# Moving the rotated rows of the rotary embedding: from a TensorE matmul to transfers inside SBUF, issued from the weight-load queue

## The chip, the cores and the metric

The kernel runs on one core of a Trainium2 chip. The metric is the device time of one execution in microseconds; a number for a kernel is the median of several executions. Lower is better.

## The reference

Two layers of a first kind, then two of a second kind, on a sequence of 512 tokens and a width of 1024. Only the first kind is touched. Each such layer projects x with `w_in`, turns four of the projected parts (queries and key of the sparse attention, queries and key of its index) by the rotary embedding, and goes on with three kinds of attention, a merge, a feed-forward part and normalizations.

```python
def rope(x, pos):
    half = x.shape[-1] // 2
    inv = ROPE_THETA ** (-jnp.arange(half, dtype=jnp.float32) / half)
    ang = pos.astype(jnp.float32)[:, None] * inv[None, :]
    cos, sin = ...                      # of ang, broadcast over heads
    x1, x2 = x[..., :half], x[..., half:]
    return jnp.concatenate([x1 * cos - x2 * sin, x2 * cos + x1 * sin], axis=-1)

for i in range(DEPTH):                  # first_block, DEPTH = 2
    h = x @ w_in[i]
    (fq, fk, fv, ff_logit, sq, sk, sv, dq, dk, dv, iq, ik, iw, g) = split_cols(h)
    ...
    dq, dk, iq, ik = rope(dq), rope(dk), rope(iq), rope(ik)    # heads of 64
    o_dsa = dsa_attention(dq, dk, dv, iq, ik, iw)
    ...
```

A rotated row is the row of the other half of the same head of 64: row r is paired with row r XOR 32, and the pairing carries a minus sign for the lower half.

## The kernel before

Everything is kept with features on partitions and the 512 tokens along the free dimension. Weights come in *units*: 1024 inputs by 128 outputs, one transfer of 512 KB into one of four buffers `w_raw`. ScalarE splits a unit into a rounded part `w_hi` (`act_split`, L396), GpSimd computes the rest `w_lo` (`pool_split`, L411), and TensorE multiplies a unit in 24 matmuls (`pe_tile`, L387 to L389: eight input tiles, three products each) into the PSUM bank of the unit's slot, unit number modulo 4. ScalarE then takes the bank into the tile `proj` (L1149, `take`) and at once splits the raw unit four places further on. There is no planner: each engine has a program in a fixed order, and semaphores tie them together.

The semaphores that matter: `bank_free[s]` counts that ScalarE has emptied the bank of slot s, so the projected tile stands in `proj`; `lo_ready[s]` counts that GpSimd is through with `w_raw[s]`, so that the next unit may be loaded into it; `unit_done[s]` counts that TensorE has finished a unit; `rope_done` counts tiles that VectorE has turned.

SyncE's queue, `sp_stream`, only loads weights: in a loop over groups of four units it waits for `lo_ready[s]` and issues the load of unit v, which means that unit v-4 has been split, which happens when unit v-8 has been taken out of its bank.

The projection of a first-kind layer is 25 units, in the order `A_ORDER`. The nine tiles to be turned, `ROPE`, are exactly its first nine, so tile n of `ROPE` is unit n. Three of them use 64 partitions, six use 128. `ROT_AT` says after which unit TensorE makes which rotated tiles: two after units 3, 5, 7 and 9, one after unit 10. Each is a matmul with a constant 128x128 matrix of +1 and -1 (L997), into the PSUM bank `X[n % 2]`. VectorE multiplies the tile by the cosine (L1389), the bank by the sine (L1390), and adds (L1392). The first wait for a rotated tile also releases the two VectorE operations ahead of them (L1381, L1383) that prepare the forget gate of another attention part.

Unit 0 and 1 (in the second layer unit 0, 1 and 2) are multiplied side by side, so they end close together; all later units one after another.

Of the kernel before, what the change touches and what calls it, by code (L numbers as in the profile page):

```python
# [20 lines left out]
ALU = mybir.AluOpType  # L21
# [3 lines left out]
P = 128  # L25
SEQ = 512
# [3 lines left out]
HD = 64  # L30
SLOTS = 4
DEPTH = 2
# [19 lines left out]
A_GROUPS = A_UNITS // SLOTS  # L52
# [4 lines left out]
A_ORDER = (16, 17, 18, 20, 21, 22, 23, 24, 25, 0, 1, 2, 3, 4, 5, 6, 7, 8, 9, 10, 11, 12, 13, 14, 15)  # L57
A_SPARE = 25

ROT_AT = {3: (0, 1), 5: (2, 3), 7: (4, 5), 9: (6, 7), 10: (8,)}  # L60
VT_AT = {11: (0, 1), 13: (2, 3), 15: (4, 5), 23: (6,)}
# [10 lines left out]
C_ID, C_ROT, C_TRI, C_CAUS, C_STRICT, C_ST01, C_CHUNK = (P * n for n in range(7))  # L72
# [37 lines left out]
def plan(nc, ctx):  # L110

    S = Plan()
# [99 lines left out]
    def sem(name):  # L212
        return ctx.enter_context(nc.semaphore(name))
# [10 lines left out]
    S.dup_ready = sem("dup_ready")  # L224
    S.rot_ready = sem("rot_ready")
    S.rope_done = sem("rope_done")
# [170 lines left out]


def sp_stream(S, sp, w_dram, groups):

    with sp.Fori(1, groups) as g:
        for s in range(SLOTS):
            sp.wait_ge(S.lo_ready[s], g)
            src = w_dram[bass.ds(g * SLOTS + s, 1), :, :].rearrange("a p n -> (a p) n")
            sp.dma_start(S.raw[s][:, :], src).then_inc(S.raw_landed[s], 16)

# [539 lines left out]
def GA(L, u, i=0):  # L946

    return L * A_GROUPS + u // SLOTS + i
# [33 lines left out]
def a_tensor(S, pe):  # L982
    nc = S.nc
    ident = S.con[:, C_ID:C_ID + P]
    for L in range(DEPTH):
        G = lambda u, i=0: L * A_GROUPS + u // SLOTS + i

        def taken(tile):
            u = A_ORDER.index(tile)
            pe.wait_ge(S.bank_free[u % SLOTS], G(u) + 2)  # L990

        def rot(n):
            tile = ROPE[n][0]
            taken(tile)
            if n >= 2:
                pe.wait_ge(S.rope_done, L * len(ROPE) + n - 1)
            nc.tensor.matmul(S.X[n % 2][:, :], S.con[:, C_ROT:C_ROT + P], S.qkv[:, tile * SEQ:(tile + 1) * SEQ],  # L997
                             start=True, stop=True).then_inc(S.rot_ready, 1)

        def turn_v(v):  # L1000
# [14 lines left out]
        for u in range(wide, len(A_ORDER)):  # L1015
            pe_unit(S, pe, u, G(u), S.ps[u % SLOTS][:, :], S.xh, S.xl).then_inc(S.unit_done[u % SLOTS], 1)
            if L == 0 and u == min(ROT_AT):
                pe.wait_ge(S.con_landed, 16 * 5)
            for n in ROT_AT.get(u, ()):
                rot(n)  # L1020
            for v in VT_AT.get(u, ()):
                turn_v(v)
# [49 lines left out]
        for i in range(2):  # L1072
            for jj in range(4):
                u = A_UP + jj
# [297 lines left out]
def a_vector(S, dve):  # L1372
    nc = S.nc
    for L in range(DEPTH):
# [3 lines left out]

        dve.wait_ge(S.rot_ready, L * len(ROPE) + 1)
        f, na = S.c[64:128, :], S.wk[5][64:128, :]  # L1380
# [4 lines left out]
        for n, (u, lo, hi) in enumerate(ROPE):  # L1385
            t = S.qkv[lo:hi, u * SEQ:(u + 1) * SEQ]
            a, b = S.wk[n % 2][lo:hi, :], S.wk[2 + n % 2][lo:hi, :]
            dve.wait_ge(S.rot_ready, L * len(ROPE) + n + 1)
            nc.vector.tensor_tensor(a, t, S.cos[lo:hi, :], ALU.mult)  # L1389
            nc.vector.tensor_tensor(b, S.X[n % 2][lo:hi, :], S.sin[lo:hi, :], ALU.mult)  # L1390
            dve.drain()
            nc.vector.tensor_tensor(t, a, b, ALU.add).then_inc(S.rope_done, 1)  # L1392
# [1098 lines left out]
def rope_constants():  # L2491
    inv = np.float32(10000.0) ** (-np.arange(32, dtype=np.float32) / np.float32(32))
    ang = (np.arange(SEQ, dtype=np.float32)[:, None] * inv[None, :]).astype(np.float32)
    rep = lambda t: np.ascontiguousarray(np.tile(t.T, (4, 1)).astype(np.float32))
    return rep(np.cos(ang)), rep(np.sin(ang))

# [31 lines left out]
```

## Time and profile before

| | us |
|---|---|
| median of 3 runs | 2758.76 (2757.78 to 2759.20) |
| the profiled execution, its own time | 2759.12 |
| its span, first to last instruction | 2757.3 |
| TensorE busy in the span | 2670.7 (97%) |
| VectorE, ScalarE, GpSimd busy | 1448.3, 1143.9, 1061.0 |

The busy time of TensorE is a modelled one, since matmuls overlap; what one matmul costs is read from the distance between starts, or between the takings of two banks. The span lies 1.8 us below the execution's own time, which is 0.36 us above the median.

### The profile page before, as it was taken

The page shows a single profiled execution, that of the slowest core. Times are in us where ns is not written, and L with a number is a line of the kernel's source. Part 1 is how long each engine was busy: PE and PEld are TensorE (multiplying, and loading weights), DVE is VectorE, ACT ScalarE, POOL GpSimd, SP SyncE. Part 2 cuts the span into 40 slices and gives each one's busy share as a digit, 9 for nine tenths or more (in the row PEclk, how much of TensorE's full clock was granted, in tenths as well). Part 3 has the DMA queues.
Part 4 walks back from the last instruction along what each step waited for, and adds up shares of the span by engine and source line. Part 5 has one row for each costly group of instructions (what it writes and reads, how often), then busy time and mean ns, then how long its engine had stood idle before and what let it go on. Part 6 is the DMA issues. An engine that isn't in the chain of part 4 may idle for free.

```text
span 2757.3 us, 35837 instructions
## 1 busy us (share of the span) xinstructions
PE 2670.7 (97%) x12688; PEld 2034.4 (74%) x12688; DVE 1448.3 (53%) x2434; ACT 1143.9 (41%) x1984; POOL 1061.0 (38%) x430
## 2 busy tenths in 40 slices
PE   8999999999999999999999999999999999999998
PEld 6867666688888778676667888886787766887766
DVE  5237647463223252486374533233688764688764
ACT  2344445243223342454444332324336554337554
POOL 4332123344444334321133444453346622347612
PEclk9999999999999999999999999999999999999999
DMA  4221111233332222211122322232133211233211
GB/s 162 91 77 54 47 46 62 77 99 94 97 99 91 84 76 85 76 54 45 40 77 77 107 92 91 94 104 76 61 103 119 85 39 54 76 98 120 72 40 54
DMA packets 61322, 220.33 MB, mean 80 GB/s; under 512 B 6928, under 2 KB 7056, under 8 KB 61200
## 3 DMA queue, kind: packets, MB, share of 16 engines
q1 hardware_dynamic: 60624, 217.12, 24.5%
q8 instruction: 78, 1.28, 0.2%
q10 hardware_dynamic: 576, 1.57, 0.2%
q14 instruction: 44, 0.36, 0.0%
HBM read 216.57 MB, written 2.10 MB: 79 GB/s over the span
## 4 chain that ended last, share of the span: by engine, by line
PE 92%; DVE 3%; ACT 2%; POOL 1%; DVEq 1%; issue 1%; DMA 0%; ACTq 0%; SPq 0%
PE bank L387 25%; PE bank L389 24%; PE bank L388 24%; PE bank L501 3%; PE bank L528 3%; PE bank L514 2%; PE bank L850 1%; PE bank L716 1%; POOL w_lo L411 1%; PE bank L504 1%; PE bank L708 1%; PE bank L734 1%; PE bank L1033 1%; PE bank L738 1%; PE bank L997 1%
## 5 line engine op out<-in xcount | busy, mean ns | idle before, releaser
L411 POOL TENSOR_TENSOR w_lo<-w_raw,w_hi 128x1024 fp32r<-128x1024 f32 x404 | 1010.4, 2509 | 1666.8 <-ACT w_hi L396 1660.9
L387 PE MATMUL bank<-x_hi,w_hi 128*128 128x512 f32 x2112 | 872.7, 413 | 30.7 <-DVE x_lo L2324 11.0
L389 PE MATMUL bank<-x_hi,w_lo 128*128 128x512 f32 x2112 | 830.7, 393 | 0.0
L388 PE MATMUL bank<-x_lo,w_hi 128*128 128x512 f32 x2112 | 829.4, 393 | 0.0
L396 ACT ACTIVATE w_hi<-w_raw 128x1024 fp32r<-128x1024 f32 x400 | 419.5, 1055 | 437.9 <-PE bank L389 376.0
L387 PEld LDWEIGHTS bank<-x_hi,w_hi 128*128 128x128 f32 x2112 | 400.4, 190 | 147.4 <-issue 49.3
L389 PEld LDWEIGHTS bank<-x_hi,w_lo 128*128 128x128 f32 x2112 | 399.9, 189 | 86.5
L388 PEld LDWEIGHTS bank<-x_lo,w_hi 128*128 128x128 f32 x2112 | 401.4, 190 | 78.9 <-issue 7.2
L387 PE MATMUL bank<-rhs_hi,w_hi 128*128 128x512 f32 x624 | 245.9, 394 | 6.1 <-DVE rhs_lo L1472 6.1
L388 PE MATMUL bank<-rhs_lo,w_hi 128*128 128x512 f32 x624 | 244.2, 391 | 0.0
L389 PE MATMUL bank<-rhs_hi,w_lo 128*128 128x512 f32 x624 | 243.9, 391 | 0.0
L558 ACT ACTIVATE work<-bank,neg_max 128x128 f32<-128x128 f32 (+3 forms) x216 | 112.0, 523 | 210.4 <-DVE neg_max L586 174.5
L1537 DVE TENSOR_TENSOR ffn_sum<-ffn_sum,bank 128x512 f32 x64 | 43.9, 688 | 286.1 <-PE bank L389 286.1
L2094 DVE SCALAR_TENSOR_TENSOR bank<-glu_out,params_b_cur,bank 128x512 f32<-128x512 f32 x216 | 152.7, 752 | 35.1 <-issue 35.1
L1527 DVE TENSOR_TENSOR work<-work 128x512 f32<-128x512 f32 x64 | 90.9, 1420 | 139.6 <-ACT rhs_hi L1292 139.6
L387 PEld LDWEIGHTS bank<-rhs_hi,w_hi 128*128 128x128 f32 x624 | 117.7, 189 | 36.2 <-issue 11.7
L389 PEld LDWEIGHTS bank<-rhs_hi,w_lo 128*128 128x128 f32 x624 | 118.0, 189 | 24.7
L388 PEld LDWEIGHTS bank<-rhs_lo,w_hi 128*128 128x128 f32 x624 | 118.0, 189 | 23.9
L586 DVE TENSOR_REDUCE neg_max<-bank 128x1 f32<-128x128 f32 (+3 forms) x216 | 96.1, 484 | 64.2 <-PE bank L504 62.6
L1290 ACT ACTIVATE work<-bank 128x512 f32<-128x512 f32 x64 | 38.0, 594 | 193.3 <-PE bank L389 185.1
L1149 ACT ACTIVATE proj<-bank 128x512 f32<-128x512 f32 x50 | 29.9, 597 | 201.7 <-PE bank L389 201.7
L567 ACT ACTIVATE work<-bank 128x128 f32<-128x128 f32 (+3 forms) x216 | 82.8, 437 | 41.9 <-PE bank L528 32.7
(391 smaller groups left out, 3257.7 us busy)
## 6 DMA issues: line engine op xcount, KB each, us to landing
w_raw<-w SPq DMA_DIRECT2D x404, 512.0 KB, 3.5
ln_in<-x SPq DMA_DIRECT2D x4, 512.0 KB, 7.4
out<-residual SPq DMA_DIRECT2D x8, 256.0 KB, 2.2
p_raw<-p ACTq DMA_DIRECT2D x2, 512.0 KB, 3.6
constants<-con SPq DMA_DIRECT2D x1, 455.0 KB, 10.3
cos<-cos SPq DMA_DIRECT2D x1, 256.0 KB, 10.4
sin<-sin SPq DMA_DIRECT2D x1, 256.0 KB, 10.2
params_b<-prm_b ACTq DMA_DIRECT2D x1, 256.0 KB, 3.7
```

Source lines behind the costliest of these rows:

```text
L387: nc.tensor.matmul(out, wh, xh, start=first, stop=False)
L388: nc.tensor.matmul(out, wh, xl, start=False, stop=False)
L389: S.last = nc.tensor.matmul(out, wl, xh, start=False, stop=last)
L396: S.nc.scalar.activation(S.wh[s][:, :], S.raw[s][:, :], ACT.Copy).then_inc(S.hi_ready[s], 1)
L411: S.nc.gpsimd.tensor_tensor(S.wl[s][:, :], S.raw[s][:, :], S.wh[s][:, :].bitcast(F32), ALU.subtract).then_inc(S.lo_ready[s], 1)
L501: nc.tensor.matmul(S.X[e][:, 0:h.w], q, k, start=True, stop=False, skip_group_check=True)
L528: m = nc.tensor.matmul(h.bank[half(e), h.b * P:h.w], v, p, start=(h.begins and x == 0), stop=(h.ends and x == len(terms) - 1), skip_group_ ...
L558: nc.scalar.activation(h.probs[e][:, 0:h.w], S.X[e][:, 0:h.w], ACT.Exp, bias=S.nm[x][:, :], accum_out=S.rs2[:, x:x + 1]).then_inc(Z.p, 1)
L567: nc.scalar.activation(h.turned[e][:, 0:h.w], (S.X[2], S.ps[2])[e][:, 0:h.w], ACT.Copy).then_inc(Z.ptc, 1)
L586: nc.vector.tensor_reduce(S.nm[2 * h.par + e][:, :], S.X[e][:, 0:h.w], AX, ALU.max, negate=True).then_inc(Z.max, 1)
L1527: nc.vector.tensor_tensor(h, S.wk[j % 2][:, :], S.wk[j % 2][:, :], ALU.mult)
L2094: stt(out=S.X[t % 2][:, :], in0=S.uc[:, bass.ds(i * 3 + (k + t * UC_W), SEQ)], scalar=S.curB[:, bass.ds(i * 3 + (k + PB_DW + t * CONV_K), ...
```

## The change

The nine rotation matmuls of each first-kind layer go. In their place SyncE's queue copies the rows within SBUF: for each tile of `ROPE` two or four transfers of 32 partitions by 512 f32 (64 KB), from `proj` into the work tile `wk[2 + n % 2]`, which VectorE then multiplies in place by the sine. The sign stands in the sine table of the host. The transfers of tile n stand ahead of the load of unit n + 8 of the layer (`ROT_LAG`), for which that part of the load loop is written out; the rest stays a loop.

```diff
-ROT_AT = {3: (0, 1), 5: (2, 3), 7: (4, 5), 9: (6, 7), 10: (8,)}
+ROT_LAG = 8
...
+def rot_count(L, n):
+
+    rows = lambda tiles: sum(hi - lo for _, lo, hi in tiles)
+    return 16 * (L * rows(ROPE[n % 2::2]) + rows(ROPE[n % 2:n + 1:2])) // 32
+
+
+def sp_rot(S, sp, L, n):
+
+    tile, lo, hi = ROPE[n]
+    u = A_ORDER.index(tile)
+    sp.wait_ge(S.bank_free[u % SLOTS], GA(L, u) + 2)
+    if n >= 2:
+        sp.wait_ge(S.rope_done, L * len(ROPE) + n - 1)
+    for r in range(lo, hi, 32):
+        other = r ^ 32
+        sp.dma_start(S.wk[2 + n % 2][r:r + 32, :], S.qkv[other:other + 32, tile * SEQ:(tile + 1) * SEQ]).then_inc(S.rot_landed[n % 2], 16)
...
 def sp_stream(S, sp, w_dram, groups):
...
+    done = 1
+    for L in range(DEPTH):
+        first, last = L * A_GROUPS + ROT_LAG // SLOTS, L * A_GROUPS + -(-(ROT_LAG + len(ROPE)) // SLOTS)
+        loads(done, first)
+        for g in range(first, last):
+            for s in range(SLOTS):
+                n = (g - L * A_GROUPS) * SLOTS + s - ROT_LAG
+                if n < len(ROPE):
+                    sp_rot(S, sp, L, n)
+                load(s, g, slice(g * SLOTS + s, g * SLOTS + s + 1))
+        done = last
+    loads(done, groups)
...
-        def rot(n):
-            tile = ROPE[n][0]
-            taken(tile)
-            if n >= 2:
-                pe.wait_ge(S.rope_done, L * len(ROPE) + n - 1)
-            nc.tensor.matmul(S.X[n % 2][:, :], S.con[:, C_ROT:C_ROT + P], S.qkv[:, tile * SEQ:(tile + 1) * SEQ],
-                             start=True, stop=True).then_inc(S.rot_ready, 1)
...
-            if L == 0 and u == min(ROT_AT):
+            if L == 0 and u == min(VT_AT):
                 pe.wait_ge(S.con_landed, 16 * 5)
-            for n in ROT_AT.get(u, ()):
-                rot(n)
...
-        dve.wait_ge(S.rot_ready, L * len(ROPE) + 1)
+        dve.wait_ge(S.rot_landed[0], rot_count(L, 0))
...
-            dve.wait_ge(S.rot_ready, L * len(ROPE) + n + 1)
+            dve.wait_ge(S.rot_landed[n % 2], rot_count(L, n))
             nc.vector.tensor_tensor(a, t, S.cos[lo:hi, :], ALU.mult)
-            nc.vector.tensor_tensor(b, S.X[n % 2][lo:hi, :], S.sin[lo:hi, :], ALU.mult)
+            nc.vector.tensor_tensor(b, b, S.sin[lo:hi, :], ALU.mult)
...
-    return rep(np.cos(ang)), rep(np.sin(ang))
+    sign = np.where(np.arange(P) % HD < HD // 2, -1, 1).astype(np.float32)[:, None]
+    return rep(np.cos(ang)), rep(np.sin(ang)) * sign
```

TensorE, before, at the end of unit 3 of the first layer (`w_hi_56` is slot 3, `w_hi_53` slot 0, so unit 4):

```order
L387 MATMUL bank<-x_hi,w_hi_56 128x512
L388 MATMUL bank<-x_lo,w_hi_56 128x512
L389 MATMUL bank<-x_hi,w_lo_60 128x512
L997 MATMUL bank<-proj,constants 128x512 [waits rope_done,bank_free0]
L997 MATMUL bank<-proj,constants 128x512 [waits rope_done,bank_free1]
L387 MATMUL bank<-x_hi,w_hi_53 128x512 [waits bank_free0,lo_ready0]
```

TensorE, of the change, at the same place (its lines are two higher):

```order
L389 MATMUL bank<-x_hi,w_hi_56 128x512
L390 MATMUL bank<-x_lo,w_hi_56 128x512
L391 MATMUL bank<-x_hi,w_lo_60 128x512
L389 MATMUL bank<-x_hi,w_hi_53 128x512 [waits bank_free0,lo_ready0]
L390 MATMUL bank<-x_lo,w_hi_53 128x512
L391 MATMUL bank<-x_hi,w_lo_57 128x512
```

Unit 4 now follows unit 3 with nothing between them.

SyncE's queue, before, the whole loop of loads:

```order
L405 ISA [waits lo_ready0]
L405 DMA w_raw_49<-w 128x1024
L405 ISA [waits lo_ready1]
L405 DMA w_raw_50<-w 128x1024
L405 ISA [waits lo_ready2]
L405 DMA w_raw_51<-w 128x1024
L405 ISA [waits lo_ready3]
L405 DMA w_raw_52<-w 128x1024
L401 REGISTER_ALU
L401 COMPARE_AND_BRANCH
```

SyncE's queue, of the change, for tiles 0 to 3 and units 8 to 11 of a layer (`work_95` and `work_96` are `wk[2]` and `wk[3]`):

```order
L416 DMA work_95<-proj 32x512 [waits bank_free0]
L416 DMA work_95<-proj 32x512
L423 DMA w_raw_49<-w 128x1024 [waits lo_ready0]
L416 DMA work_96<-proj 32x512 [waits bank_free1]
L416 DMA work_96<-proj 32x512
L423 DMA w_raw_50<-w 128x1024 [waits lo_ready1]
L416 DMA work_95<-proj 32x512 [waits rope_done,bank_free2]
L416 DMA work_95<-proj 32x512
L423 DMA w_raw_51<-w 128x1024 [waits lo_ready2]
L416 DMA work_96<-proj 32x512 [waits rope_done,bank_free3]
L416 DMA work_96<-proj 32x512 x3
L423 DMA w_raw_52<-w 128x1024 [waits lo_ready3]
```

Each of nine weight loads per layer now stands behind two or four transfers, and behind two waits that the queue did not have.

VectorE, before, the turning of tile 3 and the first row of tile 4:

```order
L1389 TENSOR_TENSOR work_94<-proj,cos 128x512 [waits rot_ready]
L1390 TENSOR_TENSOR work_96<-bank,sin 128x512
L1392 TENSOR_TENSOR proj<-work_94,work_96 128x512
L1389 TENSOR_TENSOR work_93<-proj,cos 128x512 [waits rot_ready]
L1390 TENSOR_TENSOR work_95<-bank,sin 128x512
```

VectorE, of the change, at the same place:

```order
L1415 TENSOR_TENSOR work_94<-proj,cos 128x512 [waits rot_landed1]
L1416 TENSOR_TENSOR work_96<-work_96,sin 128x512
L1418 TENSOR_TENSOR proj<-work_94,work_96 128x512
L1415 TENSOR_TENSOR work_93<-proj,cos 128x512 [waits rot_landed0]
L1416 TENSOR_TENSOR work_95<-work_95,sin 128x512
```

The number of VectorE's operations stays; the product with the sine reads two SBUF tiles instead of a PSUM bank and a tile.

## Rows read from the trace of the kernel before

**Rows 1.** The page: busy shares, granted clock, chain that ended last by engine.

```profile
PE 2670.7 (97%) x12688; PEld 2034.4 (74%) x12688; DVE 1448.3 (53%) x2434; ACT 1143.9 (41%) x1984; POOL 1061.0 (38%) x430
...
PEclk9999999999999999999999999999999999999999
...
PE 92%; DVE 3%; ACT 2%; POOL 1%; DVEq 1%; issue 1%; DMA 0%; ACTq 0%; SPq 0%
```

**Rows 2.** The instructions of L997 (durations min/median/max in ns, first and last start).

```profile
L997 PE MATMUL bank<-proj,constants x36: 590/591/593, 37.9 to 1039.8; 128*128 128x512 f32 x36
```

**Rows 3.** The chain that ended last, L997 in layer 0: start, us, what.

```profile
38.03 1.72 PE bank L997 x4
...
83.17 0.86 PE bank L997 x2
```

**Rows 4.** ScalarE's timeline, takings of units 4 to 7, 10 and 11.

```profile
45.27 0.60 ACT L1149 ACTIVATE proj<-bank 128x512 f32<-128x512 f32 x1 [5.67 <-PE bank L389]
...
50.71 0.60 ACT L1149 ACTIVATE proj<-bank 128x512 f32<-128x512 f32 x1 [3.89 <-PE bank L389]
...
57.92 0.60 ACT L1149 ACTIVATE proj<-bank 128x512 f32<-128x512 f32 x1 [3.02 <-PE bank L389]
...
63.36 0.60 ACT L1149 ACTIVATE proj<-bank 128x512 f32<-128x512 f32 x1 [3.76 <-PE bank L389]
...
83.21 0.60 ACT L1149 ACTIVATE proj<-bank 128x512 f32<-128x512 f32 x1 [5.53 <-PE bank L389]
...
89.56 0.60 ACT L1149 ACTIVATE proj<-bank 128x512 f32<-128x512 f32 x1 [4.81 <-PE bank L389]
```

**Rows 5.** A stretch: us; PE, PEld, DVE, ACT, POOL busy; clock; DMA share; GB/s.

```profile
130.40:135.80 5.40, 5.40 (x25) 4.49 (x24) 0.00 (x0) 1.51 (x3) 2.39 (x1) 1.00 0.31 92
```

**Rows 6.** Who waited for whom, 26 to 166 us: total, times, longest.

```profile
ACT proj L1149 <- PE bank L389: 105.7, 24, 12.8
...
DVE tick L2025 <- ACT proj L1149: 52.3, 1, 52.3
```

**Rows 7.** The load queue: its wait, its issue times, landing (min/median/max).

```profile
SPq L405 <- POOL w_lo L411: 101.7, 18, 13.0
...
42.62 0.33 SPq L405 DMA_DIRECT2D w_raw<-w  x1
...
DMA to landing us min/median/max: 3.2/3.5/9.6
```

**Rows 8.** Timeline at the start of layer 1, ScalarE, GpSimd, SyncE's queue, VectorE.

```profile
987.65 0.60 ACT L1149 ACTIVATE proj<-bank 128x512 f32<-128x512 f32 x1 [7.82 <-PE bank L389]
...
994.45 0.60 ACT L1149 ACTIVATE proj<-bank 128x512 f32<-128x512 f32 x1 [2.39 <-PE bank L389]
...
1001.66 0.60 ACT L1149 ACTIVATE proj<-bank 128x512 f32<-128x512 f32 x1 [5.67 <-PE bank L389]
...
989.28 9.63 POOL L411 TENSOR_TENSOR w_lo<-w_raw,w_hi 128x1024 fp32r<-128x1024 f32 x4 [20.99 <-ACT w_hi L396]
...
991.86 0.33 SPq L405 DMA_DIRECT2D w_raw<-w  x1
...
995.31 1.33 DVE L1381 TENSOR_SCALAR log_f_sum<-proj,params_cur 64x512 f32<-64x512 f32 x1 [14.48 <-PE bank L997]
996.71 2.74 DVE L1383 SCALAR_TENSOR_TENSOR work<-log_f_sum 64x512 f32<-64x512 f32 x1
```

**Rows 9.** Durations in ns, min/median/max: VectorE's products (layer 0), GpSimd's splits (all).

```profile
L1389 DVE TENSOR_TENSOR work<-proj,cos x9: 677/692/2782, 40.2 to 84.1; 128x512 f32<-128x512 f32 x6, 64x512 f32<-64x512 f32 x3
L1390 DVE TENSOR_TENSOR work<-bank,sin x9: 672/684/695, 42.9 to 84.7; 128x512 f32<-128x512 f32 x6, 64x512 f32<-64x512 f32 x3
...
L411 POOL TENSOR_TENSOR w_lo<-w_raw,w_hi x404: 2338/2400/3406, 5.8 to 2745.4; 128x1024 fp32r<-128x1024 f32 x135
```

**Rows 10.** DMA issues of the page: KB each, median us to landing.

```profile
out<-residual SPq DMA_DIRECT2D x8, 256.0 KB, 2.2
...
constants<-con SPq DMA_DIRECT2D x1, 455.0 KB, 10.3
```

More of the change, by code:

```diff
@@ L224, in plan @@
     S.dup_ready = sem("dup_ready")
-    S.rot_ready = sem("rot_ready")
+    S.rot_landed = [sem(f"rot_landed{e}") for e in range(2)]
     S.rope_done = sem("rope_done")
@@ L396, in act_split, with load, loads @@
     S.nc.scalar.activation(S.wh[s][:, :], S.raw[s][:, :], ACT.Copy).then_inc(S.hi_ready[s], 1)
-def sp_stream(S, sp, w_dram, groups):
[L401 to L405, printed above, removed]
+def rot_count(L, n):
[10 more added lines that the diff above has]
+        sp.dma_start(S.wk[2 + n % 2][r:r + 32, :], S.qkv[other:other + 32, tile * SEQ:(tile + 1) * SEQ]).then_inc(S.rot_landed[n % 2], 16)
+def sp_stream(S, sp, w_dram, groups):
+    def load(s, g, index):
+        sp.wait_ge(S.lo_ready[s], g)
+        sp.dma_start(S.raw[s][:, :], w_dram[index, :, :].rearrange("a p n -> (a p) n")).then_inc(S.raw_landed[s], 16)
+    def loads(first, last):
+        with sp.Fori(first, last) as g:
+            for s in range(SLOTS):
+                load(s, g, bass.ds(g * SLOTS + s, 1))
+    done = 1
[3 more added lines that the diff above has]
+        for g in range(first, last):
+            for s in range(SLOTS):
+                n = (g - L * A_GROUPS) * SLOTS + s - ROT_LAG
[4 more added lines that the diff above has]
+    loads(done, groups)
 def pool_split(S, pool, s, g):
```

## The prediction, made before the changed kernel ran

> **What bounds the kernel now.** I read the page first. TensorE is busy for 97% of the span and holds 92% of the chain of work that ended last, and its granted clock stands at the top digit in every slice [rows 1]. So time taken off TensorE's own program comes off the end, unless something else is ready too late to take its place. The question is whether this holds in the stage of the change, the projection of a first-kind layer (layer 0 from 26 us on, layer 1 up to its first taking at 987.65 us and on [rows 8]). There I read the waits: ScalarE waits for TensorE's units in all its 24 waits at L1149, 105.7 us in total [rows 6], so TensorE sets the pace, and nobody who feeds it does. A stretch without rotations shows the same from the other side: in 5.4 us TensorE is never idle, at a granted clock of 1.00 (the 2.4 GHz level), while ScalarE works 1.51 us and GpSimd 2.39 us [rows 5]. Each of these two could keep up with units of half the length.
>
> **What is removed.** Eighteen rotations in the two layers, seen as 36 matmuls of 590 ns [rows 2]; these overlap, so their sum isn't the cost. I take the distance between two takings of banks. Units 4 to 5 and 6 to 7, with no rotation between them, lie 50.71 - 45.27 = 5.44 and 63.36 - 57.92 = 5.44 us apart. Units 5 to 6, with two rotations, lie 57.92 - 50.71 = 7.21 us apart. Two rotations cost 1.77 us. Units 10 to 11, with one, lie 89.56 - 83.21 = 6.35 us apart: 0.91 us [rows 4]. A layer has four pairs and one single: 4 x 1.77 + 0.91 = 7.99 us. The chain of waits counts the same pieces at 1.72 and 0.86 us, 4 x 1.72 + 0.86 = 7.74 us [rows 3]; the 0.25 us between the two lie in the matmuls just behind a rotation. Layer 1 repeats the pattern: units 3 to 4 lie 1001.66 - 994.45 = 7.21 us apart there [rows 8]. I take 2 x 7.99 = 16.0 us, with 15.5 us as the lower bound. All other sync of TensorE is unchanged; the wait for the constants moves from unit 3 to unit 11, long after they have landed (issued before 10 us, 10.3 us to landing [rows 10]).
>
> **What is added, and what hides it.** No row shows a transfer from SBUF to SBUF, so I bound it. Below: the nearest in kind is the store of 256 KB out of SBUF, 2.2 us from issue to landing [rows 10]; a copy of 64 KB is smaller, and I take 2.2 us for the group of a tile. Above: the loads of 512 KB land in 3.5 us, at worst 9.6 us [rows 7], and the constants, queued behind others at the start, took 10.3 us [rows 10]. An issue is 0.33 us on the queue plus a little, I count 0.4 [rows 7]: 0.8 us for tiles 0 to 2, 1.6 us for the six others.
>
> Three things could make this visible.
>
> (a) *The queue.* Behind each tile's transfers stands the load of unit n + 8, and behind it all other loads. But that load waits for GpSimd's split of unit n + 4, which starts only after unit n has left its bank, and the transfers wait for the same taking: ScalarE's taking and split (1.51 us) and GpSimd's split (2.39 us) lie in between [rows 5], room for the 1.6 us of issues. The queue waited 101.7 us in 18 waits between 20 and 130 us [rows 7]. In layer 0 the load of unit 11 was issued at 42.62 and had landed by 46.1; it is needed 0.5 us behind the taking of unit 7, which the change brings from 63.36 to 59.8 [rows 4, 7]: a spare of 14 us.
>
> (b) *The second wait*, on VectorE having turned tile n - 2. It is tightest in layer 1, where three units end together. Tile 0 stands at 987.65 + 0.60 = 988.25; with 0.8 us of issues and 2.2 us it has landed at 991.3. VectorE does the forget pair, 1.33 + 2.74 us [rows 8], to 995.4, then three operations for tile 0, between 3 x 0.7 and 3 x 2.8 us [rows 9]: done between 997.5 and 1003.8. The transfers of tile 2 (0.8 us) and load 10 (3.5 us) follow: landed between 1001.8 and 1008.1. It is needed behind the taking of unit 6, 994.45 + 3 x 5.44 + 0.5 = 1011.3. The spare is 3 to 9 us. Before, this load went out near 996.5, when the third of GpSimd's four splits, 9.63 / 4 = 2.4 us each from 989.28, was over [rows 8]; loads 8 and 9 wait for that alone (the first went out at 991.86). From there on, a loop from tile n to tile n + 2 takes 1.6 + 2.2 + 2.1 to 3.8 us, against two units of TensorE, 10.9 us; the spare grows by 3.3 us or more each time. Cost: nothing.
>
> (c) *VectorE.* It gets its first tile earlier than now, since the copy needs only unit 0, and the matmul stood behind unit 3. The product with the sine reads two SBUF tiles now instead of a PSUM bank. The rows show what that may cost: the product with the cosine has two SBUF inputs, 692 ns in the median but up to 2782 ns; the one from the bank never took more than 695 ns; and GpSimd's split went up to 3406 ns where its median is 2400 [rows 9]. So up to 2.1 us more per tile on VectorE, 19 us per layer, and perhaps 0.4 to 1 us on a split. VectorE then waited 52.3 us for the end of the stage [rows 6], and GpSimd is idle for more than half of it [rows 5]: nothing of it reaches TensorE.
>
> **The sum.** 0 + 0 + 0 - 16.0 us against the profiled execution's own 2759.1 us gives 2743.1; it lay 0.36 us above the median, so 2758.8 - 16.0 = 2742.8 us. Everything behind the stage waits for TensorE or has been ready for long, and only shifts.
>
> **The rivals.**
>
> *The transfers of a tile land one after another, and weights come late in layer 1.* The landing would be four times 2.2 = 8.8 us for the large tiles and 4.4 us for the small ones. Loads 10, 12, 14 and 16 hang on one chain through tiles 0, 2, 4 and 6: 2.2 + 2.2 + 6.6 + 6.6 = 17.6 us later, against a spare of 3 to 9 us plus three times 3.3 us, so 13 to 19. Layer 1 would lose up to 4.6 us, layer 0, with some ten more to spare, nothing: 2743 to 2747.5 us. For it: nothing shows four small transfers at once; against it: thirteen issued back to back at the start all landed within some 10 us of issue, constants at 10.3 [rows 10], so they overlapped. The Trainium skill speaks against the change here: DMA: Bandwidth & Descriptors, "Rules for kernel authors", has transfers under 64 KB as mostly overhead, and two transfers to disjoint partition halves as serialized. No row before shows a pair of this kind; its fit of 2.0 us plus bytes / 436e3 gives an estimate of 2.15 us for 64 KB, and by it, fully serialized, this same case.
>
> *The same chain, but landings as slow as at the start: slower.* One mechanism, the queue held by the wait for a turned tile. With d us more per landing, load 16 is 4d late against a spare of about 16 us in layer 1 and 26 in layer 0. The change turns slower where (4d - 16) + (4d - 26) exceeds 16, at d = 7.3, a landing of 9.5 us per tile. At 10.3 us, d = 8.1, it is 16.4 + 6.4 - 16.0 = 6.8 us slower: 2765.6 us. Against it: the 10.3 us are those of a start with over 4 MB queued [rows 10]; here a load is the only neighbour, and it lands in 3.5 us [rows 7].
>
> *Nothing changes.* The stage would have to be held by something other than TensorE, or the gain be taken by a later stage that waits for something not moved: 2758.8 us. Against it speak the 5.44 us of the units without rotation [rows 4] and the waits [rows 6]; a loss of half of it, 2751 us, is as unlikely.
>
> **How the numbers follow.** Forecast 0.86, its own range 2741.3 to 2744.3 (scatter of the runs, and 15.5 us as the lower bound). Serialized transfers with some loss 0.06. Half or nothing gained 0.05, of which 0.03 lies within 0.2%. Slower 0.03. 0.2%, 5.5 us, is about what a measurement of this kernel can tell from no change; the first two cases, and what is left of the third, are faster by more. Range 2740.5 to 2748.5.
>
> **What would show it.** L997's shape in the first-kind layers is gone from the trace. Takings of units 3 to 11 lie 5.44 us apart. The stage is 8.0 us shorter in each layer, and the rest keeps its length. The transfers land in 2 to 3 us; the loads of units 8 to 16 are issued within 2 us of where they were, against their units; ScalarE never waits for `w_raw` there. The product with the sine has some instances above 2 us. VectorE is through with the tiles before unit 11 is taken. I am wrong if TensorE shows a wait for GpSimd's `w_lo` in units 8 to 20 of layer 1, or if the landing of a tile takes over 6 us, or if a later stage grows.

## The result, and the profile after

The changed kernel takes 2741.77 us (median of 4 runs, 2740.95 to 2742.50) against 2758.88 us for the kernel before, run beside it: ratio 0.9939, 95% interval 0.9921 to 0.9956, a gain of 17.1 us where 16.0 were predicted. Measured a second time beside the kernel before (*again*, below), it takes 2743.04 against 2758.31 us: 15.3 us. The profiled execution took 2740.95 us, its span is 2739.1 us (before: 2757.3), 18.2 us shorter.

Lines have moved. The taking of a bank is L1175 (was L1149), the split on GpSimd L447 (L411), the load L423 (L405), the transfers are L416, their wait for a turned tile L413, VectorE's three operations of a tile L1415, L1416, L1418 (L1389, L1390, L1392), the forget pair L1407 and L1409.

The page, in the same parts as [rows 1]:

```profile
PE 2652.0 (97%) x12646; PEld 2026.2 (74%) x12652; DVE 1458.0 (53%) x2434; ACT 1144.1 (42%) x1984; POOL 1063.3 (39%) x430
...
PEclk9999999999999999999999999999999999999999
...
PE 92%; DVE 3%; ACT 2%; POOL 1%; DVEq 1%; issue 1%; DMA 0%; ACTq 0%; SPq 0%
```

TensorE's busy time fell by 18.7 us, VectorE's rose by 10. TensorE still holds 92% of the chain that ended last: nothing took its place. ScalarE's timeline in layer 0, the takings of units 5 to 11 and of unit 12:

```profile
48.22 0.60 ACT L1175 ACTIVATE proj<-bank 128x512 f32<-128x512 f32 x1 [3.89 <-PE bank L391]
53.66 0.60 ACT L1175 ACTIVATE proj<-bank 128x512 f32<-128x512 f32 x1 [1.25 <-PE bank L391]
59.10 0.60 ACT L1175 ACTIVATE proj<-bank 128x512 f32<-128x512 f32 x1 [3.76 <-PE bank L391]
...
80.86 0.60 ACT L1175 ACTIVATE proj<-bank 128x512 f32<-128x512 f32 x1 [3.90 <-PE bank L391]
87.19 0.60 ACT L1175 ACTIVATE proj<-bank 128x512 f32<-128x512 f32 x1 [4.78 <-PE bank L391]
```

Every distance up to unit 11 is 5.44 us, also the one that was 7.21 [rows 4]. From the taking of unit 0 (26.50 before, 25.78 now) to that of unit 11 (89.56 and 80.86) it took 63.06 us, now 55.08: 7.98 us less. In layer 1, from unit 3 to unit 11, 51.50 and 43.53 us: 7.97 us less.

The transfers (durations in ns, then who waited for them in us and times, then issue to landing), and whom ScalarE and VectorE waited for in the stage, in layer 0 (26 to 160 us) first and then in layer 1 (970 to 1100 us):

```profile
L416 SPq DMA_DIRECT2D work<-proj x60: 507/590/1639, 26.4 to 1016.7; - x60
...
DMA to landing us min/median/max: 1.9/2.4/5.0
```

```profile
ACT proj L1175 <- PE bank L391: 97.3, 24, 12.4
...
DVE tick L2051 <- ACT proj L1175: 58.5, 1, 58.5
...
DVE work L1415 <- DMA work<-proj: 12.2, 5, 4.4
```

```profile
ACT proj L1175 <- PE bank L391: 82.2, 22, 6.4
...
DVE tick L2051 <- ACT proj L1175: 53.3, 1, 53.3
```

As before [rows 6], ScalarE waits for TensorE at nearly every taking (24 of 25 in layer 0); in neither stage does it wait for `w_raw`, or TensorE for `w_lo`. VectorE waits for transfers, and still has 58.5 us to spare at the end of the stage.

Layer 1 is where it is tightest. SyncE's queue, then VectorE's timeline, with what became of [rows 8]:

```profile
978.45 1.17 SPq L416 DMA_DIRECT2D work<-proj  x2
981.89 0.34 SPq L423 DMA_DIRECT2D w_raw<-w  x1
982.27 1.37 SPq L416 DMA_DIRECT2D work<-proj  x2
984.42 0.34 SPq L423 DMA_DIRECT2D w_raw<-w  x1
991.38 1.14 SPq L416 DMA_DIRECT2D work<-proj  x2
992.56 0.58 SPq L423 DMA_DIRECT2D w_raw<-w  x1
995.66 2.41 SPq L416 DMA_DIRECT2D work<-proj  x4
998.12 0.58 SPq L423 DMA_DIRECT2D w_raw<-w  x1
```

```profile
982.22 2.73 DVE L1409 SCALAR_TENSOR_TENSOR work<-log_f_sum 64x512 f32<-64x512 f32 x1
984.98 2.77 DVE L1415 TENSOR_TENSOR work<-proj,cos 64x512 f32<-64x512 f32 x1
987.67 2.87 DVE L1416 TENSOR_TENSOR work<-work,sin 64x512 f32<-64x512 f32 x1
990.62 0.68 DVE L1418 TENSOR_TENSOR proj<-work,work 64x512 f32<-64x512 f32 x1
...
994.90 0.69 DVE L1418 TENSOR_TENSOR proj<-work,work 64x512 f32<-64x512 f32 x1
```

The transfers of tile 2 stand still from 984.8 to 991.38, until VectorE has turned tile 0 (990.62 + 0.68). Load 10 behind them goes out at 992.56, lands 3.8 us later, at 996.4, and ScalarE splits it at 1001.57, right behind the taking of unit 6: a spare of 5.2 us, inside the predicted 3 to 9. But the tightest load behind a transfer is the next one. The transfers of tile 3 wait until VectorE has turned tile 1 (994.90 + 0.69); load 11 goes out at 998.12, lands 4.6 us later and is split at 1006.88: a spare of 4.2 us. Loads 12, 14 and 16 have 5.6, 9.3 and 13.8 us. A load that went out right behind transfers took 3.9 us to land in the median of 16, up to 5.7; the median of the others is 3.5.

**Where the 18.2 us came from.** 0.72 us at the very start (the first taking), 7.98 in layer 0, 7.97 in layer 1, 0.4 elsewhere, and 1.13 between the two stages, where no instruction had changed. At the start TensorE's first matmul came 0.42 us earlier (8.82 instead of 9.24), and two matmuls fewer ran at the lower clock level (14 instead of 16 of 0.60 us or more). The 1.13 us are the clock's. Ahead of layer 1's projection TensorE waits 7 us for VectorE's `x_lo` and then starts at the lower level; from its first matmul there to the first taking it took 18.02 us before and 16.61 after, 1.41 us less; 0.28 us had been lost on the way to it. The stretch right behind that wait, of the kernel before and of the kernel after (columns as in [rows 5]):

```profile
970.00:975.00 5.00, 5.00 (x13) 3.85 (x13) 4.82 (x9) 3.76 (x6) 0.00 (x0) 0.50 0.23 92
```

```profile
961.50:966.50 5.00, 5.00 (x17) 4.01 (x17) 4.82 (x9) 3.77 (x6) 0.00 (x0) 0.74 0.24 99
```

In the same five microseconds TensorE did 13 matmuls before (granted clock 0.50, the 1.2 GHz level, all through) and 17 after (0.74, so the 2.4 GHz level for half of it). That is scatter and not the change: matmul records of 0.60 us or more at this place were 13 before and 6 after, but 12 in the second profile of the changed kernel, and 11 to 14 in the nine other experiments. The first profile of the changed kernel is the odd one out.

### The profile page after: what moved, and what is told of

The parts are those of the page before. It is cut to its first block, busy times and chain, and to the rows that moved or that the text cites. A ratio compares the mean times of both kernels' runs of the same rounds, so it can differ in the third digit from the quotient of the medians.

```text
span 2739.1 us, 35746 instructions
## 1 busy us (share of the span) xinstructions
PE 2652.0 (97%) x12646; PEld 2026.2 (74%) x12652; DVE 1458.0 (53%) x2434; ACT 1144.1 (42%) x1984; POOL 1063.3 (39%) x430
## 4 chain that ended last, share of the span: by engine, by line
PE 92%; DVE 3%; ACT 2%; POOL 1%; DVEq 1%; issue 1%; DMA 0%; ACTq 0%; SPq 0%
PE bank L389 25%; PE bank L391 24%; PE bank L390 24%; PE bank L537 3%; PE bank L564 3%; PE bank L550 2%; PE bank L886 1%; PE bank L752 1%; POOL w_lo L447 1%; PE bank L744 1%; PE bank L1059 1%; PE bank L540 1%; PE bank L770 1%; PE bank L774 1%; PE bank L1610 1%
## 5 line engine op out<-in xcount | busy, mean ns | idle before, releaser
L447 POOL TENSOR_TENSOR w_lo<-w_raw,w_hi 128x1024 fp32r<-128x1024 f32 x404 | 1012.7, 2514 | 1646.4 <-ACT w_hi L398 1640.6
L389 PE MATMUL bank<-x_hi,w_hi 128*128 128x512 f32 x2112 | 867.5, 411 | 30.3 <-DVE x_lo L2350 10.6
L1175 ACT ACTIVATE proj<-bank 128x512 f32<-128x512 f32 x50 | 29.9, 598 | 183.9 <-PE bank L391 183.9
```

The lines of the kernel that those rows point to most:

```text
L389: nc.tensor.matmul(out, wh, xh, start=first, stop=False)
L447: S.nc.gpsimd.tensor_tensor(S.wl[s][:, :], S.raw[s][:, :], S.wh[s][:, :].bitcast(F32), ALU.subtract).then_inc(S.lo_ready[s], 1)
```

## The experiments

All are made from the changed kernel; ratios are to the kernel before, run on the same chip: 2757.28 us on the first (idle_both, idle_first, serial, lag4), 2758.31 on the second (double, lag12, again, both_kinds), 2758.56 on the third (both_late, b_three).

**idle_both and idle_first: is it TensorE's time alone?** The eighteen rotation matmuls come back where they stood, but turn a constant table into a bank that nobody reads, and nothing waits for them. The transfers stay.

```diff
+ROT_AT = {3: (0, 1), 5: (2, 3), 7: (4, 5), 9: (6, 7), 10: (8,)}
...
+        def rot(n):
+            tile = ROPE[n][0]
+            nc.tensor.matmul(S.X[n % 2][:, :], S.con[:, C_ROT:C_ROT + P], S.cos[:, :], start=True, stop=True)
...
-            if L == 0 and u == min(VT_AT):
+            if L == 0 and u == min(ROT_AT):
                 pe.wait_ge(S.con_landed, 16 * 5)
+            if True:
+                for n in ROT_AT.get(u, ()):
+                    rot(n)
```

In idle_first `if L == 0:` stands in place of `if True:`, so that layer 0 alone has them.

> The changed kernel with TensorE's eighteen rotation matmuls put back at their old places in both layers, but idle: they read the cosine table, wait for nothing and nobody reads their bank. The transfers stay as they are. If the gain is TensorE's own time in its program (my theory: 1.77 us for a pair, 0.91 us for the single one, 7.98 us per layer), the time is 2741.8 + 16.0 = 2757.8 us, within 0.1% of the kernel before. If the gain came from the shorter wait for the rotated tiles or from VectorE's earlier start (rival), it stays near 2742 us.

> The same idle matmuls, in the first layer only. By the first theory 2741.8 + 8.0 = 2749.8 us. The second layer then starts at another instant; the extra 1.1 to 2.1 us of the measured gain, which I put down to the moment at which TensorE's granted clock comes back after a wait at the start of layer 1 (thirteen matmuls at the lower level before, seven in the changed kernel), may come or go with it, so 2749 to 2752 us, and the count of slow matmuls there should account for what is over 8.0. By the rival (the gain isn't TensorE's time) 2742 us.

Measured: idle_both 2757.95 us, ratio 1.0002 (0.9992 to 1.0011); idle_first 2750.43 us, ratio 0.9975 (0.9965 to 0.9984). ScalarE's takings in idle_both, units 3 to 5:

```profile
36.97 0.60 ACT L1183 ACTIVATE proj<-bank 128x512 f32<-128x512 f32 x1 [3.89 <-PE bank L392]
44.18 0.60 ACT L1183 ACTIVATE proj<-bank 128x512 f32<-128x512 f32 x1 [5.66 <-PE bank L392]
49.62 0.60 ACT L1183 ACTIVATE proj<-bank 128x512 f32<-128x512 f32 x1 [3.89 <-PE bank L392]
```

The 7.21 us are back without anybody waiting for a rotation, and units 0 to 11 take the 63.06 us that they took in the kernel before. So the gain is the matmuls' own time, half of it per layer; what the waits that hung on them, the banks, VectorE's earlier start and the transfers are worth together is zero within the interval of the ratio (-2.2 to +3.0 us).

**serial: the rival of landings one after another.** Each transfer waits for the one before it to land.

```diff
-    for r in range(lo, hi, 32):
+    rows = lambda tiles: sum(hi - lo for _, lo, hi in tiles)
+    before = rot_count(L, n) - 16 * (hi - lo) // 32
+    for x, r in enumerate(range(lo, hi, 32)):
         other = r ^ 32
+        if x:
+            sp.wait_ge(S.rot_landed[n % 2], before + 16 * x)
```

> The changed kernel with a wait for each transfer's landing before the next of the same tile is issued, so that the queue is held for the sum of the landings. A large tile then holds the queue for four times 0.6 + 1.9 to 2.4 us, some 10 us, instead of 2.4 us, against 5.44 us of a unit. Six large tiles take 63 us of queue instead of 33. I expect load 16 of layer 1 some 32 us behind its need and that of layer 0 some 19 us: 2741.8 + 51 = 2793 us, 2775 to 2810, clearly slower than the kernel before, with ScalarE waiting for w_raw. By the rival that the transfers' latency is hidden anyway it stays at 2742 us; by my prediction's estimate for landings one after another, which left out that odd and even tiles share the queue, it would be 2743 to 2748 us.

Measured: 2763.02 us, ratio 1.0023 (1.0012 to 1.0034): slower than before, as the theory said, but 30 us less so. A transfer's landing is 1.9 us in the median. SyncE's queue in layer 0, and waits in layer 1 (975 to 1130 us):

```profile
49.23 8.04 SPq L420 DMA_DIRECT2D work<-proj  x4
57.31 0.58 SPq L427 DMA_DIRECT2D w_raw<-w  x1
57.99 7.86 SPq L420 DMA_DIRECT2D work<-proj  x4
65.90 0.58 SPq L427 DMA_DIRECT2D w_raw<-w  x1
```

```profile
ACT w_hi L398 <- DMA w_raw<-w: 30.9, 5, 7.3
...
PE bank L1038 <- ACT v_tok L1205: 12.7, 1, 12.7
```

A load now leaves every 8.6 us where TensorE takes a unit every 5.44 us. ScalarE waits for `w_raw`, and since it takes and splits in one fixed order, TensorE then waits 12.7 us for its `v_tok`. The landing of 1.9 us counts from the start of the issue, so a tile holds the queue for 8 us, where I had added issue and landing. By my own sum six large tiles would then take 6 x 8.6 = 52 us of queue and not 63, an estimate of 22 us less over both layers; the rest of the 30 us stays open. From the first taking of a layer to its last, layer 0 took 7.8 us longer than in the changed kernel and layer 1 15.4 us. This also shows what the rival in the prediction left out. It counted a chain through tiles 0, 2, 4 and 6 alone, but odd and even tiles share one queue: where each tile holds it for 8 us, all loads of the stage fall behind, and the change turns slower, not merely less fast. It isn't the rival itself: here the queue stands still until a transfer has landed, while in the rival only the landings would follow each other. The changed kernel shows nothing of either: the four transfers of a tile are issued within 2.41 us and each lands 2.4 us after its own issue in the median.

**lag4 and lag12: the place in the queue.** One number (and in lag4 a condition that leaves out an empty loop of loads).

```diff
-ROT_LAG = 8
+ROT_LAG = 4
```

> ROT_LAG 4 instead of 8: tile n's transfers stand ahead of the load of unit n + 4, which ScalarE wants 0.5 us behind the taking of unit n, and not ahead of the load of unit n + 8. That load now waits for the taking, the issues (1.2 or 2.4 us) and its own landing (3.5 us): from one taking to the next 0.6 + 2.4 + 3.5 + 1.05 = 7.6 us for a large tile and 6.4 for a small one, against 5.44. Nine tiles are 15.9 us more per layer, some 3 to 6 of which the weights already split hide: 2760 to 2774 us, 2767 taken, so slower than the kernel before though TensorE issues as little as in the changed one. If the place in the queue doesn't matter (rival), 2742 us.

> ROT_LAG 12 instead of 8: tile n's transfers go out some four units later, behind the load of unit n + 11. The loads behind them keep their spare, VectorE turns the tiles later, but still long before the end of the stage; ScalarE's copy at unit 8 waits for tile 2, which lands near the taking of unit 6. Expected 2741.8 us, no difference. If VectorE's early start were what gives the gain (rival), some of the 17 us is lost.

Measured: lag4 2782.16 us, ratio 1.0093 (1.0076 to 1.0110), 40 us over the changed kernel; lag12 2742.06 us, ratio 0.9943 (0.9928 to 0.9958), no difference. In lag4, the whole run's wait of the queue for a taking, ScalarE's takings in layer 0 (units 4 to 6), and waits in layer 0:

```profile
SPq L416 <- ACT proj L1176: 153.8, 18, 54.0
```

```profile
52.87 0.58 ACT L1176 ACTIVATE proj<-bank 128x512 f32<-128x512 f32 x1
60.75 0.58 ACT L1176 ACTIVATE proj<-bank 128x512 f32<-128x512 f32 x1
71.35 0.60 ACT L1176 ACTIVATE proj<-bank 128x512 f32<-128x512 f32 x1
```

```profile
ACT w_hi L398 <- DMA w_raw<-w: 52.9, 9, 6.3
...
PE bank L389 <- POOL w_lo L448: 9.9, 5, 3.3
```

With a lag of 4 the load of unit n + 4 stands behind the taking of unit n, and ScalarE splits that load before it takes unit n + 1. So the taking, the transfers, the load's landing and its split follow each other in a circle, once per unit: from the taking of unit 4 to that of unit 5 it is 7.9 us, where I had counted 7.6. ScalarE has no wait for TensorE there; the next bank is full already. Between units 5 and 6 three more instructions of ScalarE (a table load and two of the forget gate) stand in the circle, and it takes 10.6 us. The forecast of 2767 us missed by 15. Nine circles took 70.9 us in layer 0 where I had counted 64.8, with ScalarE's other instructions left out; the changed kernel needs 44.2 for them and not 9 x 5.44, since units 0 and 1 end together. Units 10 and 11, multiplied meanwhile, gave 7.9 us back. Over the whole stage that is 19.5 us more in layer 0 and 23.0 in layer 1. With 8 the queue's wait for a taking is covered by the wait for GpSimd's split that the load has anyway. With 12 the tiles come later (in the two layers together VectorE waits 45.6 us for its first tile) and nobody needs them.

The landings of all 60 transfers, in lag4 and in lag12:

```profile
DMA to landing us min/median/max: 1.9/2.0/2.8
```

```profile
DMA to landing us min/median/max: 2.5/3.3/3.8
```

In lag4 no weight load is under way when a transfer goes out, in lag12 always one. So four transfers 0.6 us apart land almost as fast as one that waits for the one before (1.9 us in serial), and the slower landings come where a load is under way.

**double: are the transfers' issues near the limit?** Every transfer is issued twice, the second copy into a work tile that nobody reads then.

```diff
-    return 16 * (L * rows(ROPE[n % 2::2]) + rows(ROPE[n % 2:n + 1:2])) // 32
+    return 2 * 16 * (L * rows(ROPE[n % 2::2]) + rows(ROPE[n % 2:n + 1:2])) // 32
...
     for r in range(lo, hi, 32):
         other = r ^ 32
+        sp.dma_start(S.wk[6 + n % 2][r:r + 32, :], S.qkv[other:other + 32, tile * SEQ:(tile + 1) * SEQ]).then_inc(S.rot_landed[n % 2], 16)
         sp.dma_start(S.wk[2 + n % 2][r:r + 32, :], S.qkv[other:other + 32, tile * SEQ:(tile + 1) * SEQ]).then_inc(S.rot_landed[n % 2], 16)
```

> The changed kernel with every transfer issued twice, the second copy into a work tile that nobody reads. The queue is busy for 8 x 0.59 + 0.58 = 5.3 us per large tile instead of 3.0, just under the 5.44 us of a unit. Expected hidden: 2741.8 us, up to 2745 if single issues are longer. If the queue's issue time were already near its limit (rival), each large tile would add 2.4 us, 28 us in all: 2770 us.

**again** is the changed kernel itself, on the same chip.

> The changed kernel once more, beside the kernel before on the same chip: 2741.8 us, 17 us below the kernel before. The profile shows again how many matmuls ran at the lower clock level at the start of layer 1; with seven of them as in the first profile the profiled run is near 2741, with thirteen near 2742.5.

Measured: double 2742.98 us, ratio 0.9942 (0.9927 to 0.9957); again 2743.04 us, ratio 0.9946 (0.9933 to 0.9960). Twice the transfers, 4.9 us of issues per large tile, cost nothing that shows, though a large tile's last copy now lands 6.3 to 7.4 us after its first issue. The room in the queue is at least double what the change uses.

**both_kinds, both_late, b_three: does it pay in the second kind of layer too?** There seven tiles (`kc`, `ks`, `kw`, four of `b_q`) are rotated by matmuls of the same size, 14 in all, so 14 x 0.88 = 12.3 us are on offer. In both_kinds all seven go by transfers of four times 64 KB; both_late moves the last four two loads later; b_three moves only the first three and leaves the matmuls of `b_q`.

```diff
+B_ROT_AT = {28: (0, 1), 31: (2,), 38: (3, 4), 40: (5, 6)}      # both_kinds: ahead of load u, the tiles
+B_ROT_AT = {28: (0, 1), 31: (2,), 40: (3, 4), 42: (5, 6)}      # both_late
+B_ROT_AT = {28: (0, 1), 31: (2,)}                              # b_three
...
+    if n < 2:
+        sp.wait_ge(S.glu_done, L * 4 + 4)
+    else:
+        sp.wait_ge(S.b_rope_done, L * NROPE + n - 1)
+    for r in range(0, P, 32):
+        other = r ^ 32
+        sp.dma_start(S.wk[6 + n % 2][r:r + 32, :], rope_tiles(S)[n][other:other + 32, :]).then_inc(S.b_rot_landed[n % 2], 16)
```

> The changed kernel with the same done in the second kind of layer: its seven rotation matmuls per layer go, the queue copies the rows (28 transfers per layer) ahead of the loads of units 28, 31, 38 and 40, and the sign stands in the constant from which the sine table is computed. Fourteen rotations at 0.89 us are 12.4 us of TensorE. If TensorE sets the pace there too: 2741.8 - 12.4 = 2729.4 us. VectorE waits 10.3 us per layer for a rotated tile there (L2143) and would wait less, but that lies beside TensorE's work. Rival: VectorE or ScalarE sets the pace in part of that stage (the convolution's 108 products per layer), so that only a part comes off: 2731 to 2738. The rotations of tiles 3 to 6 can hold the loads of units 38 to 40, since they wait for the tile before the last; then no gain, 2742.

> As both_kinds (all seven tiles of a second-kind layer by transfers), but tiles 3 to 6 stand two places later in the load queue, ahead of loads 40 and 42 in place of 38 and 40. Theory A (the loads 38 to 41 were held by the wait for a turned tile): loads 38 and 39 go out on time again, loads 40 to 43 are held less, since the tiles waited for are turned by then; part or all of the 14 x 0.88 = 12.3 us comes back: 2731 to 2742. Theory B (not the place but the chain on VectorE): 2744 to 2748, as both_kinds with 2746.2.

> The changed kernel, and in the second-kind layers the first three tiles (kc, ks, kw) turned by transfers too, ahead of the loads of units 28 and 31; the four b_q tiles keep their matmuls. Theory A (a transfer pays where no load queued behind it is held by a compute engine that is not yet through): six matmuls of about 0.88 us go, 5.3 us less than the changed kernel's 2741.8 to 2743.0, so 2736.5 to 2738; no wait of ScalarE for w_raw between 2080 and 2130 us, and the granted clock there 1.00 again. Theory B (it is the second kind's own chain, or VectorE slowed by more SBUF traffic, that took the gain in both_kinds, whichever tiles are moved): 2742 to 2746, with TensorE waiting in that stage.

Measured: both_kinds 2746.20 us, ratio 0.9957 (0.9944 to 0.9971), 3.2 us over *again* on its chip, though the two intervals overlap. both_late 2752.15 us, ratio 0.9979 (0.9970 to 0.9988), clear of the changed kernel's and above the ranges of both theories. b_three 2739.67 us, ratio 0.9932 (0.9918 to 0.9945), the lowest of all, 18.9 us below the kernel before on its chip, but its interval overlaps that of *again*.

The stage itself tells them apart better than the medians do. From GpSimd's split of one unit ahead of it to that of the unit 22 places on (2050.14 and 2166.16 us in the kernel after) it takes 116.0 us in each of the two layers, in the kernel before, the kernel after and *again* alike. In b_three it takes 114.3 and 114.4 us, in both_kinds 116.4 and 118.3, in both_late 120.8 and 120.9. So b_three gains 3.3 us of the 6 x 0.88 = 5.3 on offer, both_kinds loses 2.7 and both_late 9.7.

The queue in both_kinds, then in the kernel after, over 2085 to 2112 us:

```profile
2088.42 8.76 SPq L440 DMA_DIRECT2D work<-b_q  x8
2097.22 1.08 SPq L447 DMA_DIRECT2D w_raw<-w  x2
```

```profile
2092.66 17.61 SPq L423 DMA_DIRECT2D w_raw<-w  x6
```

Load 38 stands behind transfers that wait for VectorE to have turned a tile, and goes out 4.6 us later; ScalarE then waits 9.2 us for `w_raw`. That was my theory A, and both_late tests it: with the tiles two loads later that wait of ScalarE is gone, as expected, but the kernel is 6 us slower still where I expected a gain. What replaced it, in waits over 2050 to 2160 us of both_late, and then over 2080 to 2130 us of b_three:

```profile
ACT lru_tmp L2002 <- DVE lru_i L2194: 9.4, 1, 9.4
...
PE bank L1775 <- DVE b_q L2159: 3.9, 1, 3.9
```

```profile
PE bank L1761 <- DVE b_kw L2173: 1.8, 1, 1.8
```

The larger one is ScalarE's. VectorE's `lru_i` stands in its order behind the turning of tiles 3 and 4, and starts at 2110.01 in both_late, 12.3 us later than in the kernel after (2097.76); ScalarE waits 9.4 us for it, in each layer, which no other of these runs shows. TensorE waits for turned tiles in both. VectorE is busy for 21.1 of the 30 us from 2080 to 2110 in the kernel after (22.6 in *again*) and for 28.6 in b_three. Tile 2 in b_three, and the same tile in the kernel after:

```profile
2089.76 2.87 DVE L2165 TENSOR_TENSOR work<-b_kw,cos 128x512 f32<-128x512 f32 x1
2092.56 2.85 DVE L2168 TENSOR_TENSOR work<-work,sin 128x512 f32<-128x512 f32 x1
2095.48 0.69 DVE L2173 TENSOR_TENSOR b_kw<-work,work 128x512 f32<-128x512 f32 x1
```

```profile
2086.75 1.77 DVE L2141 TENSOR_TENSOR work<-b_kw,cos 128x512 f32<-128x512 f32 x1
2088.44 0.68 DVE L2143 TENSOR_TENSOR work<-bank,sin 128x512 f32<-128x512 f32 x1
2089.19 1.04 DVE L2145 TENSOR_TENSOR b_kw<-work,work 128x512 f32<-128x512 f32 x1
```

The product with the sine takes 2.85 us from SBUF where it took 0.68 us from the bank, and the tile is ready at 2096.2 instead of 2090.2. Of these 6.0 us, 2.4 lie ahead of the turning of tile 1 (this profile enters the stage 2.8 us later) and 3.6 in the turning of tiles 1 and 2. TensorE's waits for `b_kw` come to 3.6 us in both layers together; by these alone 1.7 of the 5.3 us would be left. The stage shows 3.3, since TensorE's wait of 0.8 us per layer for `w_lo` in the kernel after is gone in b_three. So for b_three neither theory holds as written: no load is late (A's condition), yet VectorE takes 2.0 us, more than a third, of the gain (B). In both_kinds and both_late the late tiles cost more than the matmuls, and the clock adds to it, at the 1.2 GHz level for part of 2110 to 2125 us:

```profile
2110.00:2125.00 15.00, 11.05 (x42) 8.89 (x41) 12.36 (x26) 12.59 (x13) 2.09 (x1) 0.77 0.38 123
```

(both_late; the kernel after shows 15.00 busy, 66 matmuls and 1.00 in the same stretch.) The 12.5 us between b_three and both_late lie in this stage (13.0 us by the lengths above). That they come by way of VectorE, and in both_late through ScalarE's wait for `lru_i`, is read from these waits and was not tested by a run of its own; how they divide between that wait, TensorE's own and the clock was not separated.

## Why the prediction was right, and where it was not

**What is removed**: right. 7.98 and 7.97 us against 7.99 per layer; idle_both gives the sum back whole, and serial and lag4 show that the same removal can end slower than the kernel before. The lower value from the chain of waits (7.74) was the wrong one of the two: the distance of takings holds what the chain leaves to the matmuls behind a rotation.

**(a) The queue**: right in the result, off in the size of a term. I counted 0.4 us for an issue; it is 0.59 us, so 2.4 us per large tile and not 1.6, and the load right behind it takes 0.58 us instead of 0.33 [rows 7]. double shows that this does not matter. The landing was 2.4 us in the median against 2.2, with 17 of 60 above 3 us; from a large tile's first issue to its last landing it took 3.8 to 5.5 us against 1.6 + 2.2. Load 11 of layer 0 had landed 13.0 us ahead of its split, against 14. lag4 shows that the reasoning itself carries weight: the same transfers four places earlier cost 40 us.

**(b) The second wait**: right that it costs nothing, with a spare of 5.2 us at load 10 against 3 to 9. But the sentence that loads 8 to 16 would go out within 2 us of where they were was wrong in layer 1 for loads 10 to 13: measured from the first taking they went out 5.9, 8.9, 4.9 and 2.9 us later (load 10 at 14.74 us, before at 8.9, which is 996.5 as I had placed it). My own working had load 10 2 to 8 us later; the list of signs contradicted the paragraph. The working also followed the even tiles alone. Load 11, behind tile 3 and so behind the turning of tile 1, has the smallest spare of those behind transfers, 4.2 us, and no term of mine covered it. And the loop did not gain 3.3 us each time: the 3.8 us that I took as the most for turning a tile has no row behind it (three operations of up to 2.8 us are 8.4), and from load 10 to 12, 14 and 16 the spare grew by 0.4, 3.6 and 4.5 us. That this sufficed was partly luck: no row told how many of VectorE's operations would be slow at once.

**(c) VectorE**: right, and far inside its bound. The product with the sine reaches 2.88 us where it had never passed 0.695 [rows 9], but in 3 of 18 instances, all in layer 1; the other 15 took 0.69 us or less. The three operations of all eighteen tiles took 56.9 us together, before 52.7: 4.2 us more in both layers, where I had allowed up to 19 per layer. [rows 9] left out that the add, with two SBUF inputs too, had been the slow one, 2.3 to 2.5 us in 8 of 18; it is now slow in 2. VectorE is through with the tiles at 71.1 us in layer 0, 9.8 us before unit 11 is taken, and 4.8 us before it in layer 1. The Trainium skill, SBUF — State Buffer, "Who interferes with whom", has it that a VectorE instruction with two SBUF inputs contends with a GpSimd one that reads SBUF, and one with at most one such input, outside the modes that use both ports, does not. The trace agrees (up to 2.88 us against never more than 0.695, though GpSimd's splits lay beside eight of the eighteen products from the bank as well). In the first kind the 58.5 us of slack hide it; b_three shows the same 2.2 us unhidden on tile 2.

**The rivals.** Serialized landings: not seen. Four transfers of 64 KB, issued back to back, land 2.4 us after their issue in the median, and 2.0 in lag4, where nothing else is under way; a large tile was through in 5.5 us at most, where the rival had 8.8. My working had put its price at up to 4.6 us. The Trainium skill, DMA: Bandwidth & Descriptors, "Rules for kernel authors", calls transfers under 64 KB mostly overhead and two transfers to disjoint partition halves serialized; that serialization shows in no row here. The same page's fit, from which I had estimated 2.15 us, is given there for DMAs issued by GpSimd, and these are SyncE's; the measured 1.9 us in serial lies near it all the same. Slower by the same chain: serial built a relative of it, with the queue itself held, and 8 us of hold per tile made the kernel slower than the one before. A tile's landing of 9.5 us was not seen in the changed kernel. Nothing changes: idle_both is what that looks like.

**The result's 1.1 us beyond 16.0** lies within the scatter: of the clock behind the wait for `x_lo` (up to 1.4 us) and of the start (25.26 to 26.69 us for the first taking over the runs). Over both measurements the gain is 15.3 and 17.1 us, and the forecast lies between.

## What to carry to other kernels

Small work on the engine that sets the pace comes off in full if its replacement stands in a queue ahead of an item that was waiting anyway, with more lead than one round of buffers (8 loads here; 4 cost 40 us). The same move in another stage fails where the engine that consumes the moved data (here VectorE, through operands that now come from SBUF) is itself nearly on the path, or has work behind it that another engine needs (`lru_i`), and where a wait for its progress stands ahead of everybody's loads. Read for both before moving: whose spare time at the end of the stage pays (52 us here; there TensorE and ScalarE wait for VectorE), and what else stands behind the new wait.

## What the runs showed of the hardware

- Transfers from SBUF to SBUF of 64 KB (32 partitions by 2 KB) on SyncE's queue: issue 0.51 us alone, 0.59 us back to back; landing 1.9 us at least, 2.0 in the median with no weight load under way (lag4), 3.3 with one under way each time (lag12), 2.4 in the mix of the changed kernel. A load issued right behind them took 0.58 us to issue instead of 0.34, and 3.9 us in the median to land instead of 3.5.
- A 128x512 product on VectorE with both inputs in SBUF took 0.68 us or up to 2.9 us; with one input in a PSUM bank never more than 0.695 us.
- Behind one and the same wait of 7 us TensorE did between 6 and 14 matmuls at the lower clock level, in profiles of the same kernel too (6 and 12), each some 0.2 us longer. A difference of a microsecond between two single profiles can be that alone.
